# Output projection ordered by column halves, a seventh expert-weight slot in the memory of the normalised rows, and those rows read back for the tail

## The chip, the cores and the metric

One Trainium2 chip, one core. The metric is the device time of one launch in microseconds (us), taken as the median of the runs; the profile is of one further execution of the same kernel. MB is 10^6 bytes, KB in the profile is 1024 bytes: one expert matrix of "1024.0 KB" is 1.05 MB.

## The reference, cut to what matters

```python
# x (1, 512, 1024) float32, DEPTH = 1
h = LayerNorm1(alpha * x + m @ w_out)        # m: merged output of two attention mixers, (512, 1024)
# MoE: 4 groups x 8 experts, top-1 group, top-2 experts in it, EXPERT_FF = 256
for g in range(4):
    hg = silu(h @ w_gate[g]) * (h @ w_up[g])             # per expert 1024 x 256, twice
    y = y + (hg * combine[:, g]) @ w_down[g]             # per expert 256 x 1024
out = LayerNorm2(alpha * h + y)
```

All weights are float32. Gate, up and down of one expert are 1.05 MB each, so the 32 experts are 100.7 MB that must be read once from HBM.

## The kernel before, in words

The projections and the attention fill the first 430 us and are not touched. Then come three stages.

**Output projection and first LayerNorm (L1143 to L1162 on TensorE).** The product with w_out is cut into eight units: four tiles of 128 tokens (t) times two halves of 512 columns (h). A unit is 24 matmuls (`unit`, L910: eight slices k of the contraction, three products of high and low parts each). They run token tile by token tile: unit 2t, then unit 2t+1. After both halves of a tile, VectorE adds the residual (`residual`, L1773), sums, subtracts the mean (`centre`, L1787, into the buffer z), and `norm1` (L1795) writes the normalised rows h1[t]. ScalarE computes the squares (L1508), copies the transposed rows for the router (`copy_h1t`, L1516) and scales x (`scale_x`, L1499); GpSimd computes the reciprocal root (L761, L764). Between units TensorE transposes z (`turn_z`, L1089), computes the routing logits (`router`, L1100) and the ranks of tokens inside their expert (`rank`, L1111). VectorE takes the top experts (`select`, L1804 and after), `weigh` and `place` (L1838 and after).

SyncE issues every large transfer, in program order on one queue (q1). In this stage its program is: expert 0, experts 1 and 2 (L610 to L613); then for t = 0 to 3 wait for h1[t] and store it to HBM (`h1_rows` there, L626). Before t = 2's store it waits for unit 5 and reads x[3]; before t = 3's it waits for unit 6 and issues gate 3, up 3 and down 4, waits for unit 7 and issues gate 4 and down 3. After the stores it waits for all routing and issues up 4 and expert 5.

**Experts.** Weights go through six slots (`EXS`). Block b is expert b on at most 64 of its tokens. TensorE per block: `start(b+1)` (L1229: 32 matmuls of gate and up, with the two transposes L1211 of block b's hidden rows in the middle, then the four transposes L1130 of the next rows), then `finish(b)` (L1245: 8 matmuls of down), then `after(b)` for single chores. GpSimd gathers the rows of later blocks from HBM (L782, first three L772) and scatters the results of blocks 0 to 29 to HBM (L794); each index column is copied first (L779, L789). SyncE refills: gate and up of b + 6 when block b's gate and up are done, down of b + 6 when its down is done (L634 to L655). Blocks 0 to 5 are written out; the rest run in loops. Chores: the two rows of LayerNorm2's parameters are loaded as rows (4 KB) and spread by TensorE (L1276) and ScalarE (L1582) after blocks 1 and 2; h1 is scaled by alpha in place (`scale_h1`, L1536) after blocks 1 to 4; after block 5 `h1_rows(0)` (L1261) puts alpha * h1[0] into a PSUM bank that later collects the sum.

**Tail (L1307).** For each token tile TensorE adds alpha * h1[t] (L1261), the rows of the last two blocks (L1269) and for t = 2, 3 one more row set (L1318). SyncE waits for the scatters, reads the result pairs yk (L672, eight reads of 512 KB), VectorE and ScalarE add and normalise, SyncE stores the output.

If some expert has more than 64 tokens there is an extra loop; with these inputs the `If` at L507 takes the branch without it.

Of the kernel before, what the change touches and what calls it, by code (L numbers as in the profile page):

```python
# [19 lines left out]
ALU = mybir.AluOpType  # L20
# [3 lines left out]
P = 128  # L24
# [57 lines left out]
def units():  # L82
# [10 lines left out]
    out += [("out", 2 * t + i, None, 512 * i) for t in range(TT) for i in range(2)]  # L93
# [11 lines left out]
EXS = 6  # L105
# [6 lines left out]
XGS = 3  # L112
# [3 lines left out]
SIDE_AT = (1, 2, EXS - 1)  # L116
LATE = NE - N_LATE
AHEAD = PEX + XGS

# [6 lines left out]
def bank_of(u):  # L126
    kind, i, _, _ = UNITS[u]
    if kind == "out":
        return 4 + i % 4
# [13 lines left out]
def build(nc, x, w_in, a_sinks, kv_norm_g, w_uk, w_uv, w_branch_a, w_branch_b, w_out, ln1_g, ln1_b,  # L143
          rg_w, rg_b, re_w, re_b, w_gate, w_up, w_down, ln2_g, ln2_b, out):
    ctx = ExitStack()
    with ctx:
# [8 lines left out]
        ARENA = EXS * EXW + 2 * D + DT * T + TT * D  # L155
# [86 lines left out]
        ln2g, ln2b = ln1g, ln1b  # L242
# [18 lines left out]
        ex_gu = [view(f, 2, DT, FF) for f in ex_off]  # L261
        ex_d = [view(f + 2 * DT * FF, 2, D) for f in ex_off]
        moe = ga_t[:, :, :].rearrange("p k c -> p (k c)")

        def small(off, *shape):
# [7 lines left out]
        y_sb = [small(2816 + 512 * i, 512) for i in range(2)]  # L273
        squared = [[view(r_att + 2 * D, D, dt=BF16) for t in range(TT)],
                   [view(ex_off[3] + D * t, D) for t in range(TT)]]
        centred = [view(ex_off[5] + D * t, D) for t in range(TT)]
        assert ex_off[4] == ex_off[2] + EXW
        yk = [[view(ex_off[2] + D * (2 * t + k), D) for k in range(2)] for t in range(TT)]
# [54 lines left out]
        y_late = [view(r_qb + D // 2 * i, D // 2) for i in range(N_LATE)]  # L333
        late_codes = [strip[:, 128 + TT * i:128 + TT * i + TT] for i in range(N_LATE)]
# [30 lines left out]
        w0_landed, w0_high = [sem(f"w0_landed{i}") for i in range(len(FIRST_ROWS))], sem("w0_high")  # L365
        back_split = sem("back_split")
        small_landed = sem("small_landed")
        ln1_landed, ln2_landed, x2_landed = sem("ln1_landed"), sem("ln2_landed"), [sem(f"x2_landed{t}") for t in range(TT)]
# [20 lines left out]
        merged_read, m_ready = sem("merged_read"), sem("m_ready")  # L389
# [4 lines left out]
        z_ready, pads_ready = sem("z_ready"), sem("pads_ready")  # L394
# [11 lines left out]
        ah_ready, sel_ready = sem("ah_ready"), sem("sel_ready")  # L406
        rows_done, rows_copied = sem("rows_done"), sem("rows_copied")
        gu_landed, gu_front = [sem(f"gu_landed{i}") for i in range(EXS)], sem("gu_front")
        d_landed = [sem(f"d_landed{i}") for i in range(EXS)]
# [16 lines left out]
        SUM_BANK = [6, 0, 2, 4]  # L426

# [40 lines left out]
        def unit_wait(eng, u):  # L468
# [6 lines left out]
            elif kind == "out":  # L475
                if UNITS[u][1] >= 4:
                    eng.wait_ge(r_ready, UNITS[u][1] - 3)
            elif before:
                eng.wait_ge(unit_copied, before[-1] + 1)
# [1612 lines left out]
```

## Time and profile before

| | us |
|---|---|
| median of 3 runs (757.24 to 758.32) | 757.41 |
| the profiled execution | 759.57 |
| its span on the core | 757.8 |
| TensorE busy in the span | 731.0 (96%) |
| VectorE, ScalarE, GpSimd busy | 376.3, 303.5, 255.4 |
| HBM read | 152.56 MB |

The profiled execution took 1.8 us more than its span, and 2.2 us more than the median of the runs. "DMA" in a windows row is the mean busy share of the 16 DMA engines, "PEclk" the granted TensorE clock. A busy share of TensorE near 100% does not say that it bounds: where it waits for weights the idle time stands in the timeline, in brackets, with its releaser.

### The profile page before, as it was taken

Reading aid. Unit: us, or ns where it says so; the run is one execution under the profiler, and the core shown is the slowest. Engines: PE = TensorE matmul, PEld = TensorE weight load, DVE = VectorE, ACT = ScalarE, POOL = GpSimd, SP = SyncE. Lnnn points to the kernel's source line nnn. Section 1 sums busy time; section 2 is a strip of 40 time slices with the busy share of each in tenths; the row PEclk is TensorE's granted clock in tenths of the full one; section 3 lists DMA queues with packets and bytes.
Section 4 is the critical chain, followed back from the end, with each engine's and each line's share of the span. In section 5 each row is a group of like instructions: output and inputs, shape, how many; then the busy total and the mean of one; then the engine's idle time right before and its main releaser. Section 6 shows DMA issues by size and latency. Waiting matters only on the chain.

```text
span 757.8 us, 12102 instructions
## 1 busy us (share of the span) xinstructions
PE 731.0 (96%) x4400; PEld 511.3 (67%) x4400; DVE 376.3 (50%) x1001; ACT 303.5 (40%) x614; POOL 255.4 (34%) x310
## 2 busy tenths in 40 slices
PE   7999999999999999999999999999999999997894
PEld 6965886777777777778888878754555555554442
DVE  2436998877678867664222256645511111111146
ACT  5346325777556665565232141223322222221123
POOL 4721542222222222225695200023323333333211
PEclk9999999999999999999999999999999999999998
DMA  8511242222222222224631384699999999999973
GB/s 234 168 56 56 86 138 70 70 71 70 70 70 70 70 70 70 70 70 167 222 110 63 134 360 195 231 402 413 417 413 418 417 417 417 417 416 418 412 300 155
DMA packets 60199, 161.00 MB, mean 212 GB/s; under 512 B 8666, under 2 KB 37346, under 8 KB 48116
## 3 DMA queue, kind: packets, MB, share of 16 engines
q1 hardware_dynamic: 55108, 152.31, 53.4%
q0 software_dynamic: 5040, 8.02, 2.9%
q8 instruction: 31, 0.51, 0.3%
q14 instruction: 20, 0.16, 0.1%
HBM read 152.56 MB, written 16.25 MB: 223 GB/s over the span
## 4 chain that ended last, share of the span: by engine, by line
PE 85%; DMA 6%; DVE 3%; ACT 2%; issue 2%; POOL 1%; SPq 1%; DVEq 0%; POOLq 0%; ACTq 0%
PE psum L924 38%; PE psum L1229 12%; PE psum L1245 6%; PE psum L910 6%; PE psum L999 4%; DMA arena<-in_w_up_dram 4%; PE psum L1057 3%; PE psum L1130 2%; PE psum L1035 2%; PE psum L1051 2%; PE psum L852 1%; PE psum L969 1%; PE psum L1211 1%; DMA arena<-pair_rows 1%; PE psum L1100 1%
## 5 line engine op out<-in xcount | busy, mean ns | idle before, releaser
L924 PE MATMUL psum<-arena,arena 128*128 128x512 f32 (+1 forms) x1296 | 315.1, 394 | 0.2 <-POOL arena L709 0.2
L924 PEld LDWEIGHTS psum<-arena,arena 128*128 128x128 f32 x1296 | 235.6, 188 | 58.9 <-issue 14.1
L709 POOL TENSOR_TENSOR arena<-arena,arena 128x256 fp32r<-128x256 f32 (+1 forms) x138 | 138.1, 1035 | 234.3 <-ACT arena L1339 234.3
L1229 PE MATMUL psum<-arena,gate_a_T 128*64 128x256 f32 x1024 | 123.4, 383 | 6.9 <-DMA arena<-in_w_up_dram 6.7
L1229 PEld LDWEIGHTS psum<-arena,gate_a_T 128*64 128x64 f32 x1024 | 70.8, 137 | 55.0 <-issue 25.8
L1339 ACT ACTIVATE arena<-arena 128x2048 fp32r<-128x2048 f32 x27 | 51.5, 1907 | 37.1 <-DMA arena<-in_w_branch_b_dram 24.9
L1995 DVE COPY gate_a_T<-psum 128x128 f32<-128x128 f32 x32 | 9.3, 291 | 114.3 <-PE psum L1211 114.3
L1442 ACT ACTIVATE arena<-psum 128x1024 f32<-128x1024 f32 (+3 forms) x48 | 37.1, 773 | 67.6 <-PE psum L1035 48.4
L1432 ACT ACTIVATE arena<-arena,negm 128x193 f32<-128x193 f32 (+5 forms) x128 | 62.4, 492 | 3.6 <-DVE negm L1700 3.6
L1245 PE MATMUL psum<-arena,gate_a_T 128*64 128x512 f32 x256 | 61.9, 604 | 0.4 <-DVE gate_a_T L1995 0.4
L1550 ACT ACTIVATE gate_a_T<-psum 64x256 f32<-64x256 f32 x32 | 12.1, 377 | 117.5 <-PE psum L1229 117.5
L1989 DVE SCALAR_TENSOR_TENSOR gate_a_T<-gate_a_T,psum 64x256 f32<-64x256 f32 x32 | 13.3, 415 | 58.5 <-ACT gate_a_T L1550 58.3
L1699 DVE TENSOR_REDUCE mx<-arena 128x4 f32<-128x772 f32 (+5 forms) x48 | 40.5, 843 | 1.6
L1710 DVE TENSOR_SCALAR arena<-arena,mx 128x192 f32<-128x192 f32 (+4 forms) x128 | 40.3, 368 | 1.7
L794 POOL DMA_INDIRECT pair_rows<-gate_a_T,idx x30 | 30.9, 1029 | 30.3 <-ACT gate_a_T L1561 30.3
L910 PE MATMUL psum<-arena,arena 128*128 128x512 f32 x128 | 40.5, 398 | 0.4 <-DVE merged_low L1740 0.4
L782 POOL DMA_INDIRECT arena<-h_rows,idx x30 | 31.5, 1049 | 25.6 <-POOL idx L779 25.6
L1695 DVE SCALAR_TENSOR_TENSOR arena<-arena,psum 128x128 f32<-128x128 f32 (+3 forms) x64 | 28.2, 482 | 21.3 <-PE psum L999 21.3
L779 POOL COPY idx<-tok_i 128x1 int32 (+1 forms) x30 | 5.6, 185 | 85.8 <-PE psum L1130 85.8
L1561 ACT ACTIVATE gate_a_T<-psum 128x512 f32<-128x512 f32 x30 | 17.9, 597 | 39.4 <-PE psum L1245 39.4
L999 PE MATMUL psum<-arena,arena 64*128 64x192 f32 (+4 forms) x256 | 33.3, 389 | 0.0
L1245 PEld LDWEIGHTS psum<-arena,gate_a_T 128*64 128x64 f32 x256 | 15.7, 136 | 22.5 <-issue 18.2
(258 smaller groups left out, 881.9 us busy)
## 6 DMA issues: line engine op xcount, KB each, us to landing
arena<-in_w_down_dram SPq DMA_DIRECT2D x32, 1024.0 KB, 20.8
arena<-in_w_gate_dram SPq DMA_DIRECT2D x31, 1024.0 KB, 13.6
arena<-in_w_up_dram SPq DMA_DIRECT2D x31, 1024.0 KB, 17.7
arena<-in_w_in_dram SPq DMA_DIRECT2D x19, 1024.0 KB, 5.5
pair_rows<-arena SPq DMA_DIRECT2D x16, 256.0 KB, 5.7
arena<-in_w_branch_a_dram SPq DMA_DIRECT2D x4, 1024.0 KB, 5.8
arena<-in_w_branch_b_dram SPq DMA_DIRECT2D x4, 1024.0 KB, 5.2
arena<-in_w_out_dram SPq DMA_DIRECT2D x4, 1024.0 KB, 8.1
```

Of the source, the lines that this page charges most:

```text
L709: nc.gpsimd.tensor_tensor(lo[:, k], raw[:, k], hi[:, k], ALU.subtract).then_inc(w_split, DT // n)
L782: pool.indirect_dma_start(out=xg[s], out_offset=None, in_=h1_dram, in_offset=bass.IndirectOffsetOnAxis(ap=idx[:, s:s + 1], axis=0), bounds ...
L910: ins = nc.tensor.matmul(ps, mp, wp, start=k == 0 and p == 0, stop=k == DT - 1 and p == 2)
L924: ins = nc.tensor.matmul(ps[:, columns(kind)], wp[:, k, col:col + P], xp[:, k, columns(kind)], start=k == 0 and p == 0, stop=k == DT - 1 a ...
L999: ins = nc.tensor.matmul(psum[:, 2 * (n % 2) + par, 256 * i:256 * i + w], q, k, start=True, stop=True)
L1229: ins = nc.tensor.matmul(psum[CAP * g:CAP * g + CAP, 2 + s % 2, 0:FF], xgT[s % 2][:, k % 4, k // 4, :], ex_gu[slot][:, g, k, :], start=k = ...
L1245: ins = nc.tensor.matmul(psum[CAP * half:CAP * half + CAP, 4 + s % 2, :], hidT[s % 2][:, k, :], ex_d[slot][:, k, 512 * half:512 * half + 5 ...
L1339: nc.scalar.activation(w_hi[c % RING], w_raw[c % RING], ACT.Copy).then_inc(w_high, 1)
L1432: ins = nc.scalar.activation(out, src, ACT.Exp, bias=negm[:, n % 4, h:h + 1], accum_out=den[:, n % 4, h:h + 1])
L1442: nc.scalar.activation(pt_sb[n % 2][:, 0:cols], psum[:, 4:6, :].rearrange("p b c -> p (b c)")[:, 0:cols], ACT.Copy).then_inc(pt_copied, 1)
L1699: step(V.tensor_reduce(mx[:, n % 4, 0:heads], s[:, :, w0:] if kind == "A" else s, AX.X, ALU.max))
L1710: ins = V.tensor_scalar(part, part, mx[:, n % 4, h:h + 1], None, ALU.mult)
```

## The change

The eight output units run by column halves: all four tiles of the first 512 columns, then all four of the second. The low and high parts of w_out for the first half are then free after the fourth unit. An expert slot more (`EXS = 7`): its gate and up lie in the memory of h1, its down where ln1's parameters lay. As h1 is overwritten by gate and up of expert 6, the tail uses a copy (`h1_again`) read back from HBM into slot 4, together with LayerNorm2's parameters, all issued by SyncE behind the last weights. Alpha is applied by a scaled identity (`alpha_ident`) instead of `scale_h1`. `h1_rows(0)` moves from block 5 to block 28. `norm1` leaves VectorE: ScalarE scales z into h1 (`scale_z`), GpSimd adds ln1's bias. `place` of tile 2 comes after `select` of tile 3. All blocks are written out, without loops, so GpSimd needs no index copies. yk, the squares and the centred rows of the tail get other slots.

```diff
-    out += [("out", 2 * t + i, None, 512 * i) for t in range(TT) for i in range(2)]
+    out += [("out", TT * i + t, None, 512 * i) for i in range(2) for t in range(TT)]
-EXS = 6
+EXS = 7
+TAIL_SLOT = 4
+LATE_TURN, ALPHA_AT, H1_AT = 5, 6, 28
+        ex_gu = [view(f, 2, DT, FF) for f in ex_off + [r_qa]]
+        ex_d = [view(f, 2, D) for f in [f + 2 * DT * FF for f in ex_off] + [0]]
+        ln2g, ln2b = (view(ex_off[TAIL_SLOT] + D * i, D) for i in range(2))
+        h1_again = [view(ex_off[TAIL_SLOT] + D * (2 + t), D) for t in range(TT)]
...
         @block.sync
             expert(2, 2)
+            sp.wait_ge(unit_done, UNIT["out", TT - 1] + 1)
+            gate_up(3, 3)
+            down(4, 4)
             for t in range(TT):
                 if t == TT - 1:
+                    sp.wait_ge(wo_front_read, 1)
+                    down(3, 3)
+                    up(5, 5)
+                    sp.wait_ge(unit_done, UNIT["out", 2 * TT - 1] + 1)
                     gate(4, 4)
+                    gate(5, 5)
+                    down(5, 5)
                 sp.wait_ge(h1_ready, t + 1)
                 sp.dma_start(h1_dram[2 * t * P:2 * (t + 1) * P, :].rearrange("(p h) c -> p (h c)", h=2), h1[:, t, :]
                              ).then_inc(h1_stored, 16)
+                if t == TT - 3:
+                    sp.wait_ge(unit_done, UNIT["out", 2 * TT - 2] + 1)
+                    residual_rows(TT - 1)
             sp.wait_ge(routed, TT)
             up(4, 4)
-            expert(5, 5)
+            down(6, 6)
+            sp.wait_ge(h1_stored, 16 * TT)
+            sp.wait_ge(rows_done, PEX)
+            gate_up(6, 6)
...
+            refill_gate_up(0)
+            for b in range(NE - EXS):
                 if b + 2 < NE - EXS:
+                    refill_gate_up(b + 1)
...
+                refill_down(b)
+            sp.wait_ge(d_done, NE - EXS + 1)
+            for rows, row in ((ln2g, ln2_g), (ln2b, ln2_b)):
+                sp.dma_start(rows, row[0].partition_broadcast(P)).then_inc(ln2_landed, 16)
+            for t in range(TT):
+                sp.dma_start(h1_again[t], h1_dram[2 * t * P:2 * (t + 1) * P, :].rearrange("(p h) c -> p (h c)", h=2)
+                             ).then_inc(x2_landed[t], 16)
...
         @block.gpsimd
+                pool.wait_ge(z_scaled, 2 * t + 2)
+                for h in range(2):
+                    rows = row_half(h1[:, t, :], h)
+                    ins = nc.gpsimd.tensor_tensor(rows, rows, in_half(ln1b, h), ALU.add)
+                ins.then_inc(h1_ready, 1)
...
         @block.tensor
+            for u in range(2, TT + 1):
+                unit(UNIT["out", u])
             for t in range(1, TT):
+                u = UNIT["out", TT + t]
+                unit(u, 0, 4)
                 turn_z(t - 1)
+                unit(u, 4, 6)
+                if t >= 2:
+                    rank(t - 2)
+                unit(u, 6, DT)
                 router(t - 1)
...
             def after(b):
+                if b == H1_AT:
+                    pe.wait_ge(alpha_ready, 1)
+                    pe.wait_ge(side_copied, 1)
+                    pe.wait_ge(x2_landed[0], 32)
                     h1_rows(0)
...
         @block.scalar
+            def scale_z(t):
+                act.wait_ge(rstd_ready, t + 1)
+                for h in range(2):
+                    nc.scalar.activation(row_half(h1[:, t, :], h), in_half(z, h), ACT.Copy, scale=ln[:, 0, 4, t:t + 1]
+                                         ).then_inc(z_scaled, 1)
...
         @block.vector
+            for t in range(TT - 1):
+                residual(t, 0)
             for t in range(TT):
+                if t == TT - 1:
+                    residual(t, 0)
+                residual(t, 1)
+                centre(t)
                 if t:
                     select(t - 1)
                     weigh(t - 1)
+                if 0 < t < TT - 1:
                     place(t - 1)
             select(TT - 1)
+            place(TT - 2)
             place(TT - 1)
```

## Rows read from the trace of the kernel before

**Rows 1.** The page's 40 slices: DMA busy tenths and GB/s.
```profile
DMA  8511242222222222224631384699999999999973
GB/s 234 168 56 56 86 138 70 70 71 70 70 70 70 70 70 70 70 70 167 222 110 63 134 360 195 231 402 413 417 413 418 417 417 417 417 416 418 412 300 155
```

**Rows 2.** Windows: length, busy of five engines (x), PEclk, DMA share, GB/s.
```profile
600.00:620.00 20.00, 20.00 (x144) 10.98 (x142) 3.39 (x9) 4.71 (x9) 7.38 (x12) 1.00 1.02 417
680.00:700.00 20.00, 15.63 (x104) 7.65 (x102) 2.73 (x8) 4.23 (x8) 6.55 (x12) 1.00 1.02 419
```

**Rows 3.** Timeline of TensorE, from block 25's down to block 31 and the tail.
```profile
679.79 1.94 PE L1245 MATMUL psum<-arena,gate_a_T 128*64 128x512 f32 x8
683.11 1.95 PE L1229 MATMUL psum<-arena,gate_a_T 128*64 128x256 f32 x16 [1.38 <-DMA arena<-in_w_up_dram]
...
712.43 1.94 PE L1245 MATMUL psum<-arena,gate_a_T 128*64 128x512 f32 x8
715.46 1.95 PE L1229 MATMUL psum<-arena,gate_a_T 128*64 128x256 f32 x16 [1.09 <-DMA arena<-in_w_up_dram]
...
720.27 1.94 PE L1245 MATMUL psum<-arena,gate_a_T 128*64 128x512 f32 x8
...
730.57 1.99 PE L1269 MATMUL psum<-arena,arena 64*128 64x512 f32 x8
...
746.06 1.98 PE L1318 MATMUL psum<-arena,ident 128*128 128x512 f32 x4
```

**Rows 4.** Timeline of SyncE's queue: issue time and length of the issues.
```profile
482.63 0.33 SPq L564 DMA_DIRECT2D arena<-in_w_gate_dram  x1
...
494.76 0.33 SPq L626 DMA_DIRECT2D h_rows<-arena  x1
...
703.12 4.39 SPq L581 DMA_DIRECT2D arena<-in_w_down_dram  x2
728.90 4.34 SPq L672 DMA_DIRECT2D arena<-pair_rows  x8
```

**Rows 5.** Windows of half a microsecond around the end of the weights.
```profile
722.00:722.50 0.50, 0.50 (x8) 0.31 (x6) 0.00 (x0) 0.24 (x1) 0.50 (x1) 1.00 0.87 361
725.50:726.00 0.50, 0.50 (x8) 0.29 (x6) 0.00 (x0) 0.00 (x0) 0.00 (x0) 1.00 0.82 304
727.50:728.00 0.50, 0.50 (x3) 0.16 (x2) 0.03 (x1) 0.04 (x1) 0.00 (x0) 1.00 0.12 49
```

**Rows 6.** Windows of 2.5 us in the output projection.
```profile
470.00:472.50 2.50, 2.50 (x15) 2.16 (x15) 1.64 (x10) 0.00 (x0) 0.00 (x0) 1.00 0.01 3
485.00:487.50 2.50, 2.50 (x13) 2.06 (x12) 2.15 (x15) 0.00 (x0) 0.00 (x0) 1.00 1.00 410
```

**Rows 7.** Chain of waits: start, length, what (last output unit, h1_rows(0)).
```profile
488.58 1.48 PE psum L910 x6
...
555.54 1.96 PE psum L1261 x8
```

**Rows 8.** Timeline: what makes h1 ready and who waits for its store.
```profile
428.00 4.77 POOL L750 TENSOR_TENSOR arena<-arena,arena 128x1024 fp32r<-128x1024 f32 x2 [11.87 <-ACT arena L1490]
479.53 1.09 ACT L1516 ACTIVATE arena<-psum 128x512 f32<-128x512 f32 x2 [0.93 <-PE psum L1089]
502.49 1.30 POOL L772 DMA_INDIRECT arena<-h_rows,tok_i  x1 [9.21 <-DMA h_rows<-arena]
```

**Rows 9.** Windows of 3 us, at the start and the end.
```profile
9.00:12.00 3.00, 2.56 (x10) 2.01 (x9) 0.69 (x1) 1.63 (x3) 0.82 (x1) 0.52 1.04 379
749.00:752.00 3.00, 0.00 (x0) 0.00 (x0) 2.63 (x5) 1.24 (x2) 0.22 (x1) 1.00 0.47 187
752.00:755.00 3.00, 0.00 (x0) 0.00 (x0) 1.41 (x2) 0.00 (x0) 0.32 (x1) 0.60 0.33 124
```

**Rows 10.** DMA issues from 400 us on.
```profile
arena<-in_ln_g_dram SPq DMA_DIRECT2D x1, 512.0 KB, 4.2
```

**Rows 11.** DMA queues from 500 to 560 us: packets, MB, share of 16 engines.
```profile
q8 instruction: 4, 0.07, 0.4%
```

More of the change, by code:

```diff
@@ L128, in bank_of @@
     if kind == "out":
[L129 removed]
+        return 4 if i == 2 * TT - 1 else 4 + i % TT
     if kind in "ab":
@@ L475, in unit_wait, with where, blocks @@
             elif kind == "out":
[L476 to L477 removed]
+                if UNITS[u][1] >= TT:
+                    eng.wait_ge(r_ready, TAKEN_IN.index(UNITS[before[-1]][1]) + 1)
             elif before:
                 eng.wait_ge(unit_copied, before[-1] + 1)
[L481 removed]
+        def where(b, i, s):
+            if i is None:
+                return b % EXS, b // EXS
+            slot = OVER_SLOTS[s - NE]
+            return slot, i + len(range(slot, NE, EXS))
+        def blocks(eng, finish, start=None, between=None, after=None, ahead=None, behind=None, tail=None, first=None,
                    alone=None, over=None):
             if start:
[L486 removed]
+                start(0, None, 0)
             if between:
                 between()
[L489 to L492 removed]
+            for b in range(NE):
+                if start and b + 1 < NE:
+                    start(b + 1, None, b + 1)
+                (finish if b + 1 < NE else alone or finish)(b, None, b)
                 if after:
                     after(b)
[L495 to L504 removed]
             eng.wait_ge(over_ready, 1)
@@ L511, in blocks @@
                     ahead()
-                with eng.Fori(NE // EXS, NBLK // EXS) as i:
-                    for s in range(NE % EXS, NE % EXS + EXS):
+                with eng.Fori(0, MAX_OVER // OVS) as i:
+                    for s in range(NE, NE + OVS):
                         if start:
-                            (first or start)(i * EXS + s, i, s)
-                        (over or alone or finish)(i * EXS + s, i, s)
+                            (first or start)(i * OVS + s, i, s)
+                        (over or alone or finish)(i * OVS + s, i, s)
                 if behind:
@@ L1320, in tail @@
                     ins.then_inc(summed, 1)
-            blocks(pe, finish, start, dst_table, unrolled=1, after=after, ahead=turn_over, behind=over_taken,
+            blocks(pe, finish, start, dst_table, after=after, ahead=turn_over, behind=over_taken,
                    first=lambda b, i, s: start(b, i, s, True), alone=alone, tail=tail)
@@ L1594, in tail @@
                     squares(1, t, mean2_ready, ssq2_ready)
-            blocks(act, finish, start, unrolled=1, after=after, ahead=copy_over, over=finish_over, tail=tail)
+            blocks(act, finish, start, after=after, ahead=copy_over, over=finish_over, tail=tail)
         @block.vector
@@ L2060, in _ @@
             at_branch = []
-            blocks(dve, expert, unrolled=1, after=after, tail=tail)
+            blocks(dve, expert, after=after, tail=tail)
 _INS = ['x', 'w_in', 'a_sinks', 'kv_norm_g', 'w_uk', 'w_uv', 'w_branch_a', 'w_branch_b', 'w_out', 'ln1_g', 'ln1_b',
```

284 lines of the change are left out of this document (119 added, 165 removed).

## The prediction

> **What bounds the kernel now.** I read the page's slices first, then windows over the expert stage, then the timeline of TensorE where the experts end, then the queue of SyncE. In the slices the DMA line is at 9 tenths and 410 to 418 GB/s from about 500 us to 720 us [rows 1]. A window in the middle has TensorE at 20.00 of 20 us and the DMA share at 1.02 [rows 2]: both look full. The timeline decides. From 683 us on the gate matmuls of each block wait for `in_w_up` [rows 3]; five such waits (at 683.11, then every 7.8 to 8.3 us, the last at 715.46) of 1.1 to 1.6 us beyond what the modelled ends show. The stock of loaded slots is used up, and the kernel goes at the pace of the transfers. Three matrices of 1.05 MB and about 0.27 MB of gathers and scatters at 417 GB/s [rows 2] are (3.15 + 0.27) / 0.417 = 8.2 us a block, which is that pace. So until the last weights land the end is set by bytes and by holes in the transfers, and after them by TensorE: blocks 30 and 31 from 715.46 to 730.57, then the tail of TensorE to 748.04, then the last VectorE work and the store to 757.8 [rows 3]. The transfers fade from 722 us; at 725.5 the share is still 0.82, at 727.5 it is 0.12 [rows 5]. I take 727 us as the time at which the last weights are in.
>
> **The change, part by part.**
>
> *A wait on TensorE behind all weights.* After block 28's down TensorE now waits for h1_again[0]. SyncE issues it after down 31, the last weight, and after the two parameter broadcasts, on the same queue. Queued behind the wait are h1_rows(0), gate and up of block 30, down of 29, all of 31, and the tail; nothing else of TensorE can run. That a transfer does not overtake here is seen in h1's last store: issued at 494.76 behind gate 4 and down 3 [rows 4], and its waiter, the gather, starts only at 502.49 [rows 8], 7.7 us later, with 2.1 MB (5 us at 417 GB/s) and its own 0.5 MB (1.3 us) ahead of that. The two last down matrices were issued from 703.12 on, 24 us before they were in [rows 4, 5], so the queue is deep when h1_again joins it. It lands three 0.52 MB transfers behind the weights: 3 x 0.524 / 0.417 = 3.8 us. For the first of them the trace has one of the same size and form, ln1's broadcast, 4.2 us from issue to landing [rows 10], so nothing odd is to be expected of the shape.
>
> The Trainium skill ("DMA: Bandwidth & Descriptors", section on queues, rings and completion order) says that descriptors of one ring are consumed in order, but that a copy may use fewer than all 16 rings, so completion is not first in, first out for an issuing engine. By that a short copy could overtake; by the store above it does not. If it did, the wait would cost nothing, which is the rival "in time" below.
>
> *The hole before the experts.* The DMA is nearly idle from 462.5 us (row at 470: share 0.01) to 482.63, where gate 3, up 3 and down 4 are issued [rows 4, 6]. With column halves these three can go at the fourth unit's end. A unit is 24 matmuls; 18 take 4.18 and 6 take 1.37 us in the chain, 5.5 us together, and the last unit ends at 488.58 + 1.48 = 490.06 [rows 7]. Counting back over eight units and the chores between them, the fourth ends at 460. So 3.15 MB move forward by 22 us. But SyncE waits for h1_ready in order, and it must store h1[2] before it may look at wo_front_read. Unit 7 now ends at 488.1, since router(2) (1.7 us) and a rank come after it. In its middle, at about 485.1, tile 2's z is turned; ScalarE copies it (1.09 us [rows 8]) and then scales z (two halves, another 1.1), to 487.6; GpSimd adds the bias: L750 took 4.77 for 2 x 1024 columns, so 2.4 us for 1024 [rows 8]. h1[2] is ready at 490, where before it was at 481. Thus down 3, up 5, gate 4, gate 5, down 5 all start at 490 and not at 482.63, and the hole opens again between 470 and 490. Bounds: the gain is 7.5 us (3.15 MB) if nothing follows later, and minus 1 if the whole delay is lost. By bytes: before, 10.9 MB were moved between 462.5 and 507.5; after, 3.15 + 0.5 + 1.0 (two stores) by 490 and 17 us x 0.40 = 6.8 after it, together 11.5. That is 0.6 MB ahead, 1.4 us; I take 1 us. Expert 6's gate and up wait for the store of h1[3], which lands at about 507, while up 4 and down 6 still run until 510: no new hole.
>
> *The seventh slot.* It holds down 6 from 497 us and gate and up from 507. While the transfers run at 417 GB/s anyway [rows 1], a deeper stock moves no byte sooner. It takes the small waits of rows 3 away from the blocks before 28 (5 to 7 us of them), but TensorE only arrives earlier at the wait for h1_again. Value 0.
>
> *Start of the experts.* VectorE loses norm1 (1.4 us) and gets select and weigh of tile 2 (3.5 us) and place of tile 2 (1.3 us) behind the last unit: block 0 starts 1 to 2 us later. Hidden: the transfers bound, and TensorE has the stall at the end as slack.
>
> *Removed chores.* Two spreads of ln2's rows (1.9 us each on TensorE), four scalings of h1 on ScalarE, GpSimd's index copies (0.2 us and 0.85 us of wait in each gather). All lie where TensorE or GpSimd have slack now; value 0. h1_rows(0) leaves block 5 and comes back behind the wait: plus 1.96 us [rows 7]. Written-out blocks need their code fetched: four code packets in 60 us at 0.4% of 16 engines [rows 11] is 3.8 us, about 1 us a packet. By the same rate some five more packets come than with loops, 5 us if one DMA engine had them all, 0.3 us if spread. I take 0 and keep 5 for the range.
>
> *The clock.* TensorE stands still from about 713 to 730. At the end of the trace the clock is 1.00 in the first 3 us without work and 0.60 in the next; at the start it is 0.52 for 3 us with 2.56 us of work done in them [rows 9]. So the blocks after the wait start at the lower level: half of about 3 us of work is lost, 1.5 us (bounds 0 and 3).
>
> *The sum.* Last weights 727 - 1 = 726; h1_again[0] at 726 + 3.8 = 729.8; h1_rows(0) 1.96; lower clock 1.5; blocks 30 and 31 as before, 730.57 - 715.46 = 15.1; then to the end as before, 757.8 - 730.57 = 27.2. Span: 729.8 + 1.96 + 1.5 + 15.1 + 27.2 = 775.6. The second path, down 29 to scatter to yk, is moved too: down 29 ends 6.75 us after block 30's start (715.46 to 722.2), that is at 740.0, its copy at 740.7, the scatter lands about 5 us later and yk is issued near 746, 2 to 3 us before TensorE ends the blocks at 748.4; before it was 728.90 against 730.57. It is not late. The median of the runs was 0.4 us under the span, so 775.6 - 0.4 = 775.2 us.
>
> **The rivals.**
>
> *In time.* h1_again[0] is there when TensorE comes, because it passes the weights or the weights are in earlier than I think. Price: h1_rows(0) in the gap before block 30, 1.96 less the 1.09 of idle [rows 3], less 1 to 5 us of earlier weights: span 753 to 758, say 755. It decides where the landing lies before about 713. To get equal with before, h1_again must land by 757.8 - 45.8 = 712, so the weights by 708; that is 19 us earlier than now, and the hole before the experts is 20 us long with the stores in it. Against it: rows 4, 5 and 8. Chance 6%.
>
> *The hole is filled better.* If h1[2] is ready by 484 and the loads follow, the gain is 6.5 to 7.5 us instead of 1: about 768. For it: 3.15 MB are issued 22 us earlier. Against it: the order of waits on SyncE. With an earlier end of the weights (723.5, if the fading belongs to scatters) even 765. Chance 20%.
>
> *Transfers are late.* Code packets on one engine, or a lower clock for longer, or the bias add on GpSimd much slower than L750, so that stores and expert 6 open a hole: 3 to 7 us more, 778 to 783. Chance 14%.
>
> *The seventh slot pays.* If TensorE and not the transfers bounded the stage, as the 96% suggest, slots and code without loops would change nothing but the wait's place, and the result would be within 0.2%. Rows 3 speak against it. Chance 2%.
>
> **How the numbers follow.** The forecast has 58%, better filled 20%, late 14%, in time 6%, no change 2%. 0.2% is about what a measurement of this kernel can tell from no change. Slower 0.92, same 0.02, faster 0.06. The range goes from 764 (better filled and an earlier end) to 783 (late); outside are mostly the 8% of the last two cases.
>
> **What would show it.** One idle stretch of TensorE of 12 to 18 us between block 28's down and h1_rows(0), ended by DMA from `h1_rows`, with the DMA share at 1 for nearly all of it. The first stores of h1[2] near 490 and gate 4 behind it. A granted clock below 1 just after the stall. Blocks before 28 with almost no wait for weights. Wrong would be: that stretch absent or under 3 us; the weights' end more than 5 us from 726; the stretch from block 30 to the end not near 42 us.

## The result, and the profile after

The changed kernel took **779.09 us** (median of 4 runs, 778.66 to 780.28); the kernel before, beside it on the same chip, took 757.52 us (4 runs, 757.24 to 758.32). The ratio is **1.0283, interval 1.0268 to 1.0297**: slower by 21.6 us, where 775.2 was forecast. The profiled execution took 779.23 us, its span is 777.5 us. In the traces, the profiled execution of before was late by 1.66 us when it issued the first expert matrix (436.95 against 435.29), in a part that the change does not touch. So a time of after in this stage answers to one 1.66 us larger of before.

The page's slices, after (they answer to [rows 1]); columns as there, PEclk is the granted clock in tenths:

```profile
PE   8999999999999999999999999899999999885395
...
PEclk9999999999999999999999999999999999999598
DMA  8412421222242221117332692899999999999653
```

The change is visible without any number: in the 37th slice TensorE's digit is down to 5 while the transfers still stand at 9; in the 38th TensorE's is 3 and the clock's 5, with the transfers at 6 for the whole slice. The timeline of TensorE there (it answers to [rows 3]; L1275 gate and up, L1291 down, L1307 `h1_rows`, L1315 the tail):

```profile
704.93 1.95 PE L1275 MATMUL psum<-arena,gate_a_T 128*64 128x256 f32 x16 [1.27 <-DMA arena<-in_w_up_dram]
...
709.75 1.94 PE L1291 MATMUL psum<-arena,gate_a_T 128*64 128x512 f32 x8
731.27 3.75 PE L1307 MATMUL psum<-arena,strip 128*128 128x256 f32 x8 [19.59 <-DMA arena<-h_rows]
734.96 2.81 PE L1275 MATMUL psum<-arena,gate_a_T 128*64 128x256 f32 x16
...
738.08 1.95 PE L1275 MATMUL psum<-arena,gate_a_T 128*64 128x256 f32 x16
...
750.93 1.99 PE L1315 MATMUL psum<-arena,arena 64*128 64x512 f32 x8
```

TensorE ends block 28 at 711.7 and then does nothing for 19.59 us, until h1's first tile has come back. What it waits for was issued long before, as SyncE's queue shows (start and length of the issues; it answers to [rows 4]):

```profile
488.11 0.32 SPq L635 DMA_DIRECT2D h_rows<-arena  x1
...
700.58 4.95 SPq L589 DMA_DIRECT2D arena<-in_w_down_dram  x2
705.57 3.43 SPq L668 DMA_DIRECT2D arena<-in_ln_g_dram  x1
...
711.28 7.27 SPq L670 DMA_DIRECT2D arena<-h_rows  x4
746.66 4.53 SPq L689 DMA_DIRECT2D arena<-pair_rows  x8
```

h1_again[0] is issued at 711.28 and lands at 731.27, 20 us later, behind the weights. Windows over the stretch (columns: length, busy of five engines (x), granted clock, DMA share, GB/s):

```profile
710.00:716.00 6.00, 1.68 (x8) 0.29 (x4) 0.43 (x2) 1.05 (x2) 2.05 (x2) 1.00 1.02 409
716.00:717.00 1.00, 0.00 (x0) 0.00 (x0) 0.00 (x0) 0.00 (x0) 0.00 (x0) 0.64 1.01 406
720.00:730.00 10.00, 0.00 (x0) 0.00 (x0) 0.00 (x0) 0.00 (x0) 0.00 (x0) 0.50 0.98 400
...
733.00:734.00 1.00, 1.00 (x4) 0.73 (x4) 0.00 (x0) 0.00 (x0) 0.00 (x0) 0.50 0.06 25
736.00:737.00 1.00, 1.00 (x10) 0.55 (x8) 0.00 (x0) 0.00 (x0) 0.00 (x0) 0.62 0.00 0
```

The five engines stand still from 720 to 730 with the DMA full. The clock goes to its lower level (1.2 of 2.4 GHz) at 716 to 717, with TensorE idle since 711.7, and is back within 736 to 737. The first two groups after the stall take 3.75 and 2.81 us instead of 1.97 and 1.95. And from the landing on hardly anything is left to move: from 731.27 to 740 only 0.23 MB move, although three more tiles of h1, 1.57 MB, were issued behind the first.

The other place is the output projection. Windows of after, then of before, over the same stretches:

```profile
462.50:485.00 22.50, 22.50 (x130) 19.09 (x129) 15.45 (x61) 10.22 (x18) 7.30 (x10) 1.00 0.41 161
485.00:510.00 25.00, 21.45 (x149) 12.28 (x149) 15.85 (x68) 7.44 (x13) 8.11 (x8) 0.93 0.85 329
...
485.00:487.50 2.50, 2.50 (x19) 2.27 (x18) 2.35 (x9) 1.49 (x2) 1.99 (x2) 1.00 0.00 0
```
```profile
462.50:485.00 22.50, 22.50 (x126) 19.19 (x126) 13.83 (x48) 5.61 (x9) 1.46 (x4) 1.00 0.26 87
485.00:510.00 25.00, 23.87 (x177) 14.30 (x175) 13.07 (x60) 5.20 (x9) 4.02 (x5) 1.00 1.01 402
```

The hole is filled in its first part (161 against 87 GB/s) and what is gained there is lost again in the second: 22.5 x 0.161 + 25 x 0.329 = 11.85 MB after, 12.01 MB before. From 485.0 to 487.5, where [rows 6] have 410 GB/s, not a byte moves, until SyncE passes the wait for h1[2] at 488.11. Counted from the first expert issue of each trace, so that the 1.66 us drop out, 26.29 MB have moved after 84 us, against 26.38 before (from windows over these stretches; experiment 5, which is the kernel before with written-out blocks, has 26.71, so 0.3 MB of such a figure can be the trace's).

### The profile page after: what moved, and what is told of

It is laid out like the page before. It is cut to its first block and busy times, and to the rows that moved or that the text cites. A ratio compares the mean times of both kernels' runs of the same rounds, so it can differ in the third digit from the quotient of the medians.

```text
span 777.5 us, 11566 instructions
## 1 busy us (share of the span) xinstructions
PE 730.6 (94%) x4392; PEld 511.3 (66%) x4392; DVE 373.3 (48%) x993; ACT 302.9 (39%) x617; POOL 253.5 (33%) x258
## 5 line engine op out<-in xcount | busy, mean ns | idle before, releaser
L1275 PE MATMUL psum<-arena,gate_a_T 128*64 128x256 f32 x1024 | 124.3, 385 | 7.7 <-DMA arena<-in_w_up_dram 7.5
L1275 PEld LDWEIGHTS psum<-arena,gate_a_T 128*64 128x64 f32 x1024 | 71.0, 137 | 56.3 <-issue 14.4
L802 POOL DMA_INDIRECT arena<-h_rows,tok_i x30 | 31.0, 1032 | 126.3 <-PE psum L1168 126.3
L1291 PE MATMUL psum<-arena,gate_a_T 128*64 128x512 f32 x256 | 61.9, 604 | 0.4 <-DVE gate_a_T L2027 0.4
L809 POOL DMA_INDIRECT pair_rows<-gate_a_T,dst_i x30 | 30.6, 1022 | 45.5 <-ACT gate_a_T L1598 43.7
L1291 PEld LDWEIGHTS psum<-arena,gate_a_T 128*64 128x64 f32 x256 | 15.7, 136 | 22.5 <-issue 18.2
L1307 PE MATMUL psum<-arena,strip 128*128 128x256 f32 x32 | 9.6, 453 | 19.6 <-DMA arena<-h_rows 19.6
```

The lines of the kernel that those rows point to most:

```text
L802: pool.indirect_dma_start(out=xg[b % XGS], out_offset=None, in_=h1_dram, in_offset=bass.IndirectOffsetOnAxis(ap=tok_i[:, b:b + 1], axis=0) ...
L1275: ins = nc.tensor.matmul(psum[CAP * g:CAP * g + CAP, 2 + s % 2, 0:FF], xgT[s % 2][:, k % 4, k // 4, :], ex_gu[slot][:, g, k, :], start=k = ...
L1291: ins = nc.tensor.matmul(psum[CAP * half:CAP * half + CAP, 4 + s % 2, :], hidT[s % 2][:, k, :], ex_d[slot][:, k, 512 * half:512 * half + 5 ...
```

## The experiments

Each is a change to the kernel after, if nothing else is said, with times beside runs of the kernel before on the same chip.

**1. The place of the wait.**

```diff
-LATE_TURN, ALPHA_AT, H1_AT = 5, 6, 28
+LATE_TURN, ALPHA_AT, H1_AT = 5, 6, NE - 1
```

> The changed kernel with h1_rows(0), and with it the wait for h1_again[0], moved from behind block 28 to behind block 31. Theory (the wait holds back blocks 30 and 31): the 19.6 us stall goes, TensorE ends block 31 near 730 us, and what is left of the wait shows there: h1_again[0] lands near 731, and the reads of yk queue behind the rest of h1_again until about 735, so the tail starts some 4 us late. About 762 us in all, 17 us less than the changed kernel's 779. Rival (the loss comes from the seventh slot's transfers, the written-out code or the new first LayerNorm, and the wait only shows it): still 775 us or more.

Measured: 763.01 us (762.22 to 764.01), ratio 1.0071 [1.0054, 1.0088]. In its timeline the wait has shrunk to 0.76 us, and nothing is behind it but the tail:

```profile
728.79 1.94 PE L1291 MATMUL psum<-arena,gate_a_T 128*64 128x512 f32 x8 [0.41 <-DVE gate_a_T L2027]
731.49 1.97 PE L1307 MATMUL psum<-arena,strip 128*128 128x256 f32 x8 [0.76 <-DMA arena<-h_rows]
```

Sixteen of the 21.6 us are not the read-back's, which lands at the same time (731.49), but those of two blocks queued behind it and of the lower clock at which they start. A residue of 5.2 us is left. Part of it shows at the last wait for weights, timeline and windows of the same kernel:

```profile
704.82 1.95 PE L1275 MATMUL psum<-arena,gate_a_T 128*64 128x256 f32 x16 [1.23 <-DMA arena<-in_w_up_dram]
...
714.07 3.07 PE L1275 MATMUL psum<-arena,gate_a_T 128*64 128x256 f32 x16 [2.50 <-DMA arena<-in_w_up_dram]
```
```profile
715.00:716.00 1.00, 1.00 (x7) 0.52 (x6) 0.00 (x0) 0.00 (x0) 0.00 (x0) 0.50 1.03 385
```

Up of expert 30 comes 9.25 us after that of expert 29, where before it is 7.85 (715.46 in [rows 3], and 707.61, left out there). It is not late for all that: counted from the first expert issue it is there after 278.5 us in both kernels; up of 29 was early. But the wait of 2.50 us is followed by the lower clock, and the group takes 3.07 us.

**2. The order on the queue.** h1_again[0] goes ahead of the two parameter broadcasts.

```diff
-            for rows, row in ((ln2g, ln2_g), (ln2b, ln2_b)):
-                sp.dma_start(rows, row[0].partition_broadcast(P)).then_inc(ln2_landed, 16)
             for t in range(TT):
                 sp.dma_start(h1_again[t], ...).then_inc(x2_landed[t], 16)
+                if t == 0:
+                    for rows, row in ((ln2g, ln2_g), (ln2b, ln2_b)):
+                        sp.dma_start(rows, row[0].partition_broadcast(P)).then_inc(ln2_landed, 16)
```

> The changed kernel with h1_again[0] issued ahead of the two parameter broadcasts instead of behind them. Theory (the read lands in the order of the queue, behind all weights): it lands 2 x 0.524 MB / 417 GB/s = 2.5 us earlier, near 728.7 us, and the time falls by 2.5 us to about 776.5. Rival (the landing is set by something else, the slowest DMA engine or the latency of a read from HBM): less than 1 us.

Measured: 776.27 us (775.3 to 776.82), ratio 1.0246 [1.0229, 1.0263].

```profile
728.49 3.48 PE L1308 MATMUL psum<-arena,strip 128*128 128x256 f32 x8 [16.99 <-DMA arena<-h_rows]
731.90 1.95 PE L1276 MATMUL psum<-arena,gate_a_T 128*64 128x256 f32 x16
```

The landing moves from 731.27 to 728.49, by 2.8 us; two transfers of 0.52 MB are 2.5 us at 417 GB/s. So a transfer ahead of it is paid by its bytes, and no whole copy overtakes. Of the 2.62 MB that stand behind h1_again[0] here, 1.17 are left when it lands; the other 1.45 had gone through before it.

**3. The clock.** TensorE is kept busy with 140 transposes of the identity while it waits.

```diff
+                    keep_awake(140)
                     pe.wait_ge(x2_landed[0], 32)
```

> The changed kernel with 140 transposes of the identity (no one reads their result) on TensorE in front of the wait for h1_again[0]. Theory (the blocks after the stall start at 1.2 GHz): the granted clock stays at 1.00, h1_rows(0) takes 1.96 and not 3.75 us, the first 16 gate and up matmuls 1.95 and not 2.81; 2.6 us less, about 776.5. Rival (those matmuls are slow because their data or PSUM banks are cold or contended): no change, 779.

Measured: 777.41 us (775.22 to 778.66), ratio 1.0249 [1.0227, 1.0271].

```profile
713.85 15.50 PE L894 MATMUL psum<-ident 128*128 128x128 f32 x140
731.57 3.67 PE L1307 MATMUL psum<-arena,strip 128*128 128x256 f32 x8 [2.22 <-DMA arena<-h_rows]
735.17 1.08 PE L1275 MATMUL psum<-arena,gate_a_T 128*64 128x256 f32 x8
```
```profile
732.00:733.00 1.00, 1.00 (x3) 0.74 (x3) 0.00 (x0) 0.00 (x0) 0.00 (x0) 0.50 0.51 209
735.00:737.00 2.00, 2.00 (x17) 1.06 (x16) 0.00 (x0) 0.00 (x0) 0.00 (x0) 1.00 0.00 0
```

The experiment is half a success. The transposes end 2.2 us before the landing, and the clock still falls, at 731 to 732, though TensorE has begun to work again; `h1_rows(0)` takes 3.67 us as before. Only the second group is spared: it begins 3.60 us after the wait ends, and at full clock. Against the kernel after that is 0.9 us of the 2.65 (3.75 + 2.81 - 1.96 - 1.95). But the filler need not be what won it: experiment 2, with no filler, has 3.48 and 1.95 in the same places, a price of 1.5 us, and this one 1.7. The medians (777.41 against 779.09) are of different chips, and the intervals of the ratios touch. That the clock costs 1.5 to 2.7 us after the stall is shown; that this filler saves any of it is not.

**4. Without the seventh slot and the read-back.** Six slots, h1 stays in its place, ln2's broadcasts behind the weights; yk, the squares and the centred rows go back to the places that they had before. `h1_rows(0)` stays behind block 28, with its wait gone.

```diff
-EXS = 7
+EXS = 6
-        ex_gu = [view(f, 2, DT, FF) for f in ex_off + [r_qa]]
+        ex_gu = [view(f, 2, DT, FF) for f in ex_off]
...
-        h1_again = [view(ex_off[TAIL_SLOT] + D * (2 + t), D) for t in range(TT)]
+        h1_again = [h1[:, t, :] for t in range(TT)]
...
-            down(6, 6)
-            sp.wait_ge(h1_stored, 16 * TT)
-            sp.wait_ge(rows_done, PEX)
-            gate_up(6, 6)
...
-            for t in range(TT):
-                sp.dma_start(h1_again[t], ...).then_inc(x2_landed[t], 16)
```

> The changed kernel without the seventh slot: six slots as before, h1 stays in its memory, nothing is read back; column halves, written-out blocks, the new first LayerNorm, alpha_ident and h1_rows(0) after block 28 stay; the parameter broadcasts go where ln1's parameters were. Theory (the seventh slot is worth nothing and its read-back costs all): about 756 us, 1 to 2 less than the kernel before from 3.15 MB of weights that fill the hole. Rival (written-out code or the later h1 costs): 760 or more. Rival (a deeper stock is worth something): slower than the kernel before by 1 to 3 us, while e1 is not.

Measured: 761.01 us (760.02 to 764.09, 6 runs), ratio 1.0052 [1.003, 1.0074]. The expectation missed by 5 us. One reason is in SyncE's queue and a window:

```profile
496.50 0.43 SPq L574 DMA_DIRECT2D arena<-in_w_up_dram  x1
508.12 0.33 SPq L570 DMA_DIRECT2D arena<-in_w_gate_dram  x1
```
```profile
505.00:510.00 5.00, 4.82 (x59) 3.37 (x57) 0.84 (x2) 1.25 (x3) 2.29 (x2) 1.00 0.85 313
```

With six slots all that may be loaded is issued by 497; the next matrix needs block 0's slot, free only at 508.12. In the first 84 us 25.79 MB move, 0.67 MB or 1.6 us less than in experiment 1, and up of expert 30 comes 280.3 us after the first expert issue, 1.8 us later than there. That is the use of the seventh slot, which the prediction had put at 0. From up 30 to the end the order is the other way round: 43.1 us against 46.7, by less clock lost and a shorter tail. So the traces say that the read-back with `h1_rows(0)` in the tail costs more than the slot gives. The medians, 2 us apart on the same chip, agree in sign only: the intervals overlap.

**5. The written-out blocks alone**, in the kernel before.

```diff
-            blocks(pe, finish, start, dst_table, unrolled=1, after=after, ...)
+            blocks(pe, finish, start, dst_table, unrolled=NE // EXS, after=after, ...)
```
(and so for ScalarE, VectorE and SyncE's refills)

> The kernel before with the blocks of TensorE, ScalarE and VectorE and SyncE's refills written out (GpSimd keeps its loops), nothing else changed. Theory (written-out code costs nothing: its fetches hide): 757.5 us, within 1 us of before. Rival (the added code packets fall on one DMA engine and every weight matrix waits for it): 2 to 4 us slower, and the end of the weights later by as much.

Measured: 758.32 us (757.38 to 760.23, 12 runs against 17 of before at 757.32), ratio 1.0018 [1.0008, 1.0028]. It costs 0.6 to 2.1 us by the interval; q8, the queue of the code, has 38 packets in the whole span against 31. That these packets are the cause is not shown. The prediction had 0.

**6. One matrix more in stock.** As experiment 4, with a place for the down of expert 6 where ln1's parameters lay; block 0's down is then not refilled.

```diff
+        ex_d6 = view(0, 2, D)
...
             up(4, 4)
+            down(EXS, 0)
```

> e4 (column halves, six slots, h1 kept) with one more place, for the down matrix of expert 6 alone, in the memory of ln1's parameters; it is issued behind up 4, and the refill of block 0's down falls away. Theory (e4 lost because its six slots were full at about 505 us and the transfers stood until block 0 gave one back): the 1.05 MB fill that hole, 2.5 us less than e4, about 758.5 us. Rival (e4's loss lies in the tail or in the code): no change against e4's 761.

Measured: 761.97 us (760.66 to 764.32), ratio 1.0062 [1.0045, 1.0078]: no gain, a miss. 26.04 MB move in the first 84 us, 0.25 more than in experiment 4 and not the 1.05 of the matrix: in its trace block 0 starts later, at 506.73 against 504.46, and hands back its slot at 510.39.

```profile
495.00:500.00 5.00, 2.96 (x19) 0.80 (x16) 4.46 (x24) 0.00 (x0) 0.97 (x1) 1.00 1.01 426
500.00:505.00 5.00, 4.68 (x32) 2.00 (x30) 2.71 (x16) 0.60 (x1) 0.00 (x0) 0.66 0.96 346
```

TensorE is idle for 2 of the 5 us before 500, waiting for VectorE's routing, and its clock is lower just after (0.66). This differs between traces of nearly the same program: the idle time is 0.3 us and block 0 starts 68.7 to 68.8 us after the first expert issue in three (experiments 1, 2, 4), 2.0 us and 70.3 to 70.7 in four (after, 3, 6, the second run of 1); before it is 66.2, at a clock of 1.00. What sorts these seven is where the clock falls. All have a gap of 1.2 to 1.5 us near 489, where TensorE waits for VectorE's L1824 ahead of eight transposes (L1125 in most of them). In the three, the clock is at its lower level from right behind the gap until about 492.5 and the transposes take 1.97 us instead of 1.32; what hangs on them, GpSimd's last two adds too, comes some 0.65 us later, behind the two small instructions of VectorE that the adds hold up by 2.0 us in the four (the rows are in the last section). In the four, the clock stays up there and falls near 499, behind the idle time of 2 us, when twelve matmuls of L1160 are next. They take 4.4 to 4.6 us, in the three 3.2. The first row is of experiment 1, the second of after:

```profile
489.58 1.97 PE L1125 MATMUL psum<-ident,arena 128*128 128x128 f32 x8 [1.21 <-DVE arena L1824]
```
```profile
498.03 4.36 PE L1160 MATMUL psum<-arena,arena 128*64 128x512 f32 x12
```

This is read off seven traces and not tried, and why the clock falls at one place or the other is open (in experiment 9 it is 0.50 from 491 to 500, and block 0 starts after 71.1 us). But a kernel of this family can have block 0 1.5 to 2 us earlier or later by it, which blurs every comparison of single traces here.

**7. norm1 back on VectorE.** As experiment 4, with GpSimd's add and ScalarE's scaling taken out.

```diff
-                pool.wait_ge(z_scaled, 2 * t + 2)
-                ... nc.gpsimd.tensor_tensor(rows, rows, in_half(ln1b, h), ALU.add)
-                scale_z(t)
+                norm1(t)
```

> e4 with h1 written by VectorE again (one pass of scale and bias) instead of ScalarE and GpSimd. Theory (VectorE's work after the last output unit sets when block 0 starts, and GpSimd's adds slow VectorE's small instructions, 1.32 us for one that takes 0.24 alone, so that both ways cost the same): within 1 us of e4's 761. Rival (the new first LayerNorm is what made block 0 late): 2 us less than e4. Rival (it was a gain): 2 us more.

Measured: 764.2 us (762.97 to 765.57), ratio 1.0087 [1.0072, 1.0102], 3.2 us more than experiment 4 (on another chip) and 2.2 more than experiment 6 on the same chip, where within 1 was expected. Block 0 starts at 507.91 and the hole is deep; 24.44 MB in the first 84 us are 1.35 MB less than in experiment 4, 3.2 us at 417 GB/s, as much as the difference of the medians:

```profile
505.00:510.00 5.00, 4.67 (x37) 2.65 (x35) 0.92 (x6) 1.60 (x3) 2.30 (x2) 1.00 0.11 27
```

Block 0 is there 71.8 us after the first expert issue, against 68.7 in experiment 4 and 70.5 in experiment 6. So with column halves work on VectorE delays block 0, and taking norm1 from it is a gain.

**8. A mixed order**, on the kernel of experiment 5: only tiles 2 and 3 are interleaved by halves, so that half of w_out is free one unit earlier, and SyncE's loads go forward with it (gate 3, up 3 and down 4 behind that unit, down 3 and up 5 in the middle of the last one); norm1 stays on VectorE, the down of expert 6 has the place of experiment 6, and ln2's broadcasts go behind the weights.

```diff
-    out += [("out", 2 * t + i, None, 512 * i) for t in range(TT) for i in range(2)]
+    out += [("out", i, None, 512 * (i % 2)) for i in (0, 1, 2, 3, 4, 6, 5, 7)]
...
+            for rows, row in ((ln2g, ln2_g), (ln2b, ln2_b)):
+                sp.dma_start(rows, row[0].partition_broadcast(P)).then_inc(ln2_landed, 16)
```

> A candidate on the kernel before: output units in the order t0h0 t0h1 t1h0 t1h1 t2h0 t3h0 t2h1 t3h1, so that gate 3, up 3 and down 4 go one unit earlier; down 3 and up 5 in the middle of the last unit; one more place for down 6 (as in e6); LayerNorm2's parameters broadcast behind the weights instead of spread; blocks written out. Theory (what counts is how many bytes are in when block 0 hands back its slot, and when it does): 1 MB more by then, block 0 about 2 us later, together 2 us faster than before, 755.5 us. Rival (the later block 0 eats it): 757 to 759.

Measured: 760.24 us (759.22 to 762.58), ratio 1.0041 [1.0025, 1.0058]. The window from 480 to 485 has the share at 1.00, and the hole is back at 505:

```profile
505.00:510.00 5.00, 4.82 (x58) 3.44 (x56) 0.84 (x2) 1.09 (x3) 2.93 (x3) 1.00 0.59 188
```

It moves 26.88 MB in the first 84 us against 26.71 in experiment 5 and is 1.9 us slower. Both end block 31 at 729.7; the loss is in the tail, 28.1 us from there to the end against 26.4. What is new there is ln2's 1.05 MB behind the weights, and a wait of 1.54 us of L1329 that experiment 5 does not have. And a wait for weights of 2.78 us costs clock as in experiment 1:

```profile
706.45 3.48 PE L1243 MATMUL psum<-arena,gate_a_T 128*64 128x256 f32 x16 [2.78 <-DMA arena<-in_w_up_dram]
...
740.83 1.98 PE L1329 MATMUL psum<-arena,ident 128*128 128x512 f32 x4 [1.54 <-ACT arena L1604]
```

**9. Loads ahead of the store.** On experiment 1 (which was run again beside it), the loads behind `wo_front_read` and unit 7 go one store earlier, so that they don't wait for GpSimd's h1[2].

```diff
             for t in range(TT):
-                if t == TT - 1:
+                if t == TT - 2:
                     sp.wait_ge(wo_front_read, 1)
```

> The kernel after with h1's rows stored in the last unit and read back in the tail, run once more as the partner of the next one. Both theories: 763, within 1 (its run before gave 763.01).

> The same, with the three loads behind the wait for the front's read (down of expert 3, up of expert 5, and those behind unit 7) issued one unit earlier, ahead of the store of h1's third tile. Theory A (the end of the transfer-bound stage is set by the time at which block 0 hands back its slot; bytes loaded before that only fill the six slots sooner, and then the transfers stand): loads restart some 5 us earlier, a hole as long opens before gate and up of expert 6 at 505 to 510, and the gain is about 1 us: 762. Theory B (a filled hole is worth its bytes wherever it is): 5 us less, 758.

Measured: the partner 763.21 us (762.79 to 765.82), as in its first run; the new one **759.97 us** (759.38 to 761.72), ratio 1.0037 [1.0024, 1.0051]. The gain of 3.2 us lies between both theories. Windows of the partner, then of the new one:

```profile
485.00:490.00 5.00, 3.84 (x27) 3.22 (x25) 3.96 (x14) 2.66 (x4) 2.57 (x2) 1.00 0.08 30
...
505.00:510.00 5.00, 5.00 (x41) 2.75 (x40) 0.00 (x0) 1.19 (x2) 1.60 (x2) 1.00 1.04 433
```
```profile
485.00:490.00 5.00, 3.79 (x29) 3.33 (x28) 4.36 (x13) 2.97 (x4) 2.58 (x2) 1.00 0.99 371
...
505.00:510.00 5.00, 5.00 (x39) 2.79 (x40) 0.04 (x1) 1.19 (x2) 2.29 (x2) 1.00 0.51 151
```

1.7 MB are won in the first window and 1.4 MB lost in the second, because expert 6's gate and up, which go into h1's memory, are issued only at 507.07. What SyncE waits for there is `rows_done`, TensorE's last product that picks rows out of h1 (L1160, which ends at 506.98), and not the fourth store, which was issued near 495.5 and landed 6.1 us later. From the view of SyncE's waits (us waited, number of waits, us of one):

```profile
SPq L644 <- PE psum L1160: 9.2, 1, 9.2
```

Over the first 84 us it is 27.13 against 26.38 MB, 0.75 MB or 1.8 us ahead; up of expert 29 comes 267.4 us after the first expert issue, where the partner has 269.6. The traces show these 2.2 us; the rest of the 3.2 is in none of their steps. So a filled hole is worth something, but more than half of it comes back as a new one. This is the fastest version with the seventh slot, and still above the kernel before.

## Why the prediction was right, and by how much it was off

The forecast (775.2, range 764 to 783, slower at 0.92) held, and by its main mechanism, the wait for a read behind all weights with two blocks queued behind it. Some smaller terms came out right by luck or not at all. Step by step:

- *Transfers bound the stage*: right. From 600 to 620 the rate is 417 GB/s as in [rows 2], and the waits for `in_w_up` are still there at 704.93; the seventh slot doesn't take them away, as the prediction had thought for the blocks before 28. They even begin sooner, at 664.03 where before the first is at 683.11.
- *The hole, 1 us sooner*: right. Up of expert 29 is there 704.93 - 435.29 = 269.6 us after the first expert issue, before 707.61 - 436.95 = 270.7. But not by more bytes: after 84 us the kernel has moved no more than before, and by up 29 less, 95.82 against 96.45 MB on q1. What differs is how much of the later copies is through when up 29 lands: 94.90 MB are queued up to it (88 matrices, x[3] and four stores), so 0.92 MB after and 1.55 before. At up 30 that is 1.42 in experiment 1 and 1.51 before, and the gain in time is gone. The forecast of 1 us is met by luck. Its steps on the queue hold: gate 3 is issued at 457.97, 459.6 on the time scale of before, where 460 was forecast. Also h1[2]: ready at 488.1, which is 489.8 on the time scale of before; 490 was forecast.
- *h1_again[0] lands three transfers behind the weights*: right in kind (experiments 1 and 2), and **the term that was mis-sized**. It failed as a time, not as an order: from up of expert 29 to the landing it was to be 729.8 - (707.61 - 1) = 23.2 us; it is 731.27 - 704.93 = 26.3, so 3.1 us more. The prediction counted the bytes ahead of the copy and stopped there, as if its last share were through when its bytes' turn has come. In the trace only 0.23 of the 1.57 MB behind it are left when it lands: 1.34 MB of later copies, 3.2 us at 417 GB/s, had gone through first. I read this so: a copy is complete with the slowest of its shares, and while the queue is deep the other engines are already at later copies. The Trainium skill ("DMA: Bandwidth & Descriptors", section on queues, rings and completion order) has the same picture, a copy split over up to 16 rings, each consumed in order by itself; the 0.23 MB agree with it, the progress of single engines was not looked at. The obvious rival is a fixed delay between the last byte and the release of the waiter. The trace of before speaks against one of 3 us: x[3], 0.52 MB alone on the queue, is issued at 476.30 and lands 3.2 us later, at 479.5; its bytes move until 479.0 (352 GB/s from 478 to 479, 4 from 479 to 480), so such a delay is 0.5 us at most. That 3.2 and 3.1 agree so well is partly luck, for the 23.2 us start at up 29, which itself lands with 0.92 or 1.55 MB of later copies through (last point), and the 727 us were read off a fading share.
- *Block 0 starts 1 to 2 us later*: it is 4.0 us (505.55 + 1.66 - 503.16) in this trace, and 2.5 to 2.6 in those of experiments 1, 2 and 4. The difference is for the most part where the clock falls (experiment 6): here it is 0.50 from 498 to 501, under the last matmuls ahead of block 0. With seven slots little depends on it: the second run of experiment 1 had block 0 1.9 us later than the first, up 29 0.4 us later, and a median of 763.21 against 763.01.
- *The seventh slot, 0*: half right. It takes no wait for weights away (704.93 above), but with it up 30 comes 1.8 us sooner than with six in the same order (experiment 4).
- *Lower clock after the stall*: 1.5 forecast, 2.65 in the trace, 1.5 and 1.7 in those of experiments 2 and 3.
- *Blocks 30 and 31*: 750.93 - 731.27 - 3.75 - 0.86 = 15.05, forecast 15.1. *Tail*: 777.5 - 750.93 = 26.6, forecast 27.2; the yk reads, issued at 746.66, were not late.
- *Written-out blocks*: 0 forecast, about 1 us in experiment 5.
- *From span to median*: 0.4 us was taken off, 1.6 had to be added (777.5 to 779.09). The profiled execution of before had a first part slower by the 1.66 us; taken from its span as a fixed beginning, that hid half of the late landing. The errors are 3.1 + 1.15 - 0.6 = 3.7 us, of the 3.9 between 775.2 and 779.09.

*Where the 21.6 us went.* Sixteen are two blocks behind a read that is last on the queue, with the lower clock behind the wait (experiment 1). The other 5.2 can be looked for in the timelines of experiments 1 and 5, each from its first expert issue (435.60, 436.09) to its end (760.8, 756.1), 325.2 against 320.0 us:

| step | exp. 1 | exp. 5 | more |
|---|---|---|---|
| first expert issue to up 29 | 269.2 | 270.6 | -1.3 |
| up 29 to up 30 | 9.25 | 7.84 | +1.4 |
| up 30 to the end of block 31 | 16.66 | 15.18 | +1.5 |
| `h1_rows(0)` with its wait, then the tail | 30.1 | 26.4 | +3.6 |

The first two rows cancel: up 30 is there after 278.5 us in experiment 1 and 278.4 in experiment 5, with the same bytes moved (99.46 and 99.54 MB on q1). So no time is lost in the transfers up to there. What is lost is 1.5 us of lower clock behind the wait for up 30, then 2.65 us for `h1_rows(0)` and its wait, and 1 us in the rest of the tail. Experiment 9 has the same steps but for the first, which is 2.2 us shorter than its partner's. Why up 29 comes early and up 30 does not stays open. The 3.1 MB behind the weights were not tried by themselves: with 1.05 MB there, up 30 comes 9.06 us after up 29 in experiment 4, but within 8.1 us in experiment 8, where TensorE does not wait for it. The table reads two traces, and they overstate: written-out code is in both columns and costs about 1 us, so by the medians experiments 1 and 5 are 4.2 us apart and not 5.2.

## What to carry to other kernels

In a stage bound by transfers, an in-order engine must not wait for a small read issued behind the last large ones, unless nothing else is queued behind that wait: price it by the bytes ahead of the read and those of later copies that get through before it is complete (1.3 to 1.5 MB in these traces). A load moved forward is worth bytes only until the slots are full; find the next thing that frees a slot (here the end of block 0's first matmuls; in experiment 9 TensorE's last reading of h1) and what delays it, before counting the hole as won. And put the waits of an issuing engine in the order in which they come true: one store ahead of the ready loads cost 3.2 us.

## What the runs showed of the hardware that was not expected

**GpSimd's adds stretch some of VectorE's operations.** The timeline of the kernel after, GpSimd and then VectorE; L1849 works on 64 f16 columns, L1875 has two inputs:

```profile
477.17 2.56 POOL L786 TENSOR_TENSOR arena<-arena,arena 128x512 f32<-128x512 f32 x2 [3.55 <-ACT arena L1558]
...
492.51 2.50 POOL L786 TENSOR_TENSOR arena<-arena,arena 128x512 f32<-128x512 f32 x2 [1.84 <-ACT arena L1558]
```
```profile
477.46 0.22 DVE L1874 TENSOR_REDUCE ranks<-strip 128x2 f32<-128x64 f32 x1
477.72 0.88 DVE L1875 TENSOR_TENSOR in_slot<-col_s,ranks 128x128 f16<-128x128 f32 x1
...
492.49 1.32 DVE L1849 TENSOR_SCALAR arena<-arena,dst_code 128x64 f16<-128x64 f16 x1
493.85 1.33 DVE L1854 TENSOR_SCALAR arena<-arena,dst_code 128x32 f16<-128x32 f16 x2
...
498.17 0.24 DVE L1849 TENSOR_SCALAR arena<-arena,dst_code 128x64 f16<-128x64 f16 x1
499.48 0.29 DVE L1875 TENSOR_TENSOR in_slot<-col_s,ranks 128x128 f16<-128x128 f32 x1
```

The same L1849 takes 0.24 us alone and 1.32 us beside the adds, and the two instructions of L1854 follow with 1.33 where they take 0.37 elsewhere; together they last as long as the two adds of 1.25 us. The reduction L1874, one input, is not touched. The Trainium skill ("SBUF — State Buffer", on the two sides of SBUF) says that the port pair shared by VectorE and GpSimd is an exclusive lock: who holds it keeps it for the whole instruction, and the other blocks. The trace agrees: the stretched instructions end with an add (493.81 and 493.76, for the first) rather than running at part speed. It costs VectorE 2.0 us here, and TensorE waits 2.04 us for VectorE's L1845 before its next rank, on the way to block 0. That wait does not set block 0 back by as much: counted from the first expert issue, L1845 is only some 0.4 us later than in experiments 1, 2 and 4, where the adds come 0.65 us later, behind L1849 and L1854, and TensorE's wait is 0.28 us. That norm1 on VectorE costs more still is experiment 7.

**The clock falls after short waits too, and after work has begun again.** In experiment 1 TensorE waits 2.50 us, starts at 714.07, and the clock is 0.50 from 715 to 718: 1.4 us are lost on top of the wait. It is so in four more traces, with waits of 2.25 (its second run), 2.32 (experiment 9), 2.50 (experiment 7) and 2.78 us (experiment 8), whose first groups take 3.2 to 3.6 us. But it is not sure to come: in experiment 6 a wait of 2.75 us is followed by a group of 1.95 us at a clock of 1.00. In the kernel before, waits of 1.09 to 1.59 us in this stage leave it at 1.00. So transfers that keep the same pace on the whole but come unevenly can cost 1.4 us: up 30 of experiment 1 is not later than before's, only the wait for it is longer.
